# 384 bytes between the weight slots and the arena of a two-block transformer kernel

## What is computed

```python
# block 1
mod = silu(c) @ w_mod + b_mod                       # 1024 x 6144, for x and for the context
hx  = modulate(rmsnorm(x), ...);  hc = modulate(rmsnorm(ctx), ...)
q, k, v, hy = split(hx @ w_in); k_c, v_c = hc @ w_k, hc @ w_v
attn = (softmax(q1 k1) - lam * softmax(q2 k2)) @ v   # 4 heads, 768 keys
z    = hyena: two gated long convolutions by DFT matrices
x    = x + g_a * (concat(attn, z) @ w_out)
x    = x + g_f * ((gelu(conv3(h @ w_up_a)) * (h @ w_up_b)) @ w_down)      # 2816 wide
# block 2
x    = x + concat(hgrn2 both directions, mlstm both directions) @ w_out_2  # from x @ w_in_2
x    = x + cross_attention(x, mem)                                         # 4 heads, 256 keys
x    = x + relu(h @ w_up_2)**2 @ w_down_2                                  # 4096 wide
out  = rmsnorm(x)
```

## Time and profile before

| | |
|---|---|
| median of 3 runs | 1662.15 us (1659.91 to 1662.8) |
| profiled execution, first to last instruction | 1660.1 us |
| PE matmul busy | 1614.1 us, 97% |
| PE weight load busy | 1268.9 us, 76% |
| VectorE, ScalarE, GpSimd busy | 977.3, 682.4, 153.4 us |
| DMA | 173.89 MB, mean 105 GB/s |
| granted clock of TensorE, mean | 0.993 |

### The profile page before, as it was taken

The page is one execution under the profiler, slowest core; times in us unless marked ns, Lnnn a source line. Parts: engine busy times, 40 slices in busy tenths (PEclk is TensorE's granted clock), DMA queues, the critical chain, the costliest instruction groups (busy, mean ns, idle before and its releaser), DMA issues.

```text
span 1660.1 us, 18984 instructions
## 1 busy us (share of the span) xinstructions
PE 1614.1 (97%) x7258; PEld 1268.9 (76%) x7258; DVE 977.3 (59%) x1411; ACT 682.4 (41%) x1060; POOL 153.4 (9%) x155
## 2 busy tenths in 40 slices
PE   5999999999999999999999999999999999999997
PEld 1488765687788888888888787688877888888885
DVE  6986687784544424436789498675434554435262
ACT  4531465323533213325654667964433322222131
POOL 0221000252000000004000000342001000000001
PEclk9999999999999999999999999999999999999999
DMA  9543114422332232223141121444210322222231
GB/s 311 198 152 127 64 54 162 153 65 89 103 101 89 76 116 84 92 95 133 52 176 56 47 77 36 162 152 153 101 52 28 125 74 83 98 101 101 101 101 51
DMA packets 112600, 173.89 MB, mean 105 GB/s; under 512 B 3851, under 2 KB 56651, under 8 KB 112012
## 3 DMA queue, kind: packets, MB, share of 16 engines
q1 hardware_dynamic: 108220, 158.05, 28.2%
q0 software_dynamic: 4304, 14.81, 2.7%
HBM read 168.53 MB, written 4.33 MB: 104 GB/s over the span
## 4 chain that ended last, share of the span: by engine, by line
PE 84%; DVE 8%; DMA 3%; ACT 2%; issue 2%; SPq 1%; DVEq 0%; ACTq 0%
PE bank L902 17%; PE bank L904 17%; PE bank L903 17%; PE bank L939 6%; PE bank L940 6%; PE bank L944 5%; DMA weight_slots<-in_w_mod 2%; PE bank L1212 2%; PE bank L1132 1%; PE bank L1144 1%; PE bank L1342 1%; DVE weight_slots_lo L2435 1%; PE bank L1432 1%; PE bank L1407 1%; PE bank L1450 1%
## 5 line engine op out<-in xcount | busy, mean ns | idle before, releaser
L3328 POOL TENSOR_TENSOR arena<-arena 128x512 f32<-128x512 f32 (+1 forms) x56 | 76.3, 1371 | 960.3 <-ACT arena L1695 956.8
L904 PE MATMUL bank<-hx_hi,weight_slots_lo 128*128 128x512 f32 x320 | 124.8, 390 | 0.0
L3283 DVE TENSOR_TENSOR weight_slots_lo<-weight_slots,weights_hi 128x2048 fp32r<-128x2048 f32 x30 | 67.4, 2289 | 93.5 <-ACT weights_hi L2394 93.5
L2394 ACT ACTIVATE weights_hi<-weight_slots 128x2048 fp32r<-128x2048 f32 x30 | 55.8, 1908 | 160.6 <-DMA weight_slots<-in_w_up 115.9
L1664 ACT ACTIVATE weights_hi<-weight_slots 128x2048 fp32r<-128x2048 f32 (+2 forms) x46 | 77.3, 1724 | 91.7 <-DMA weight_slots<-in_ffn_w_down 57.9
L903 PE MATMUL bank<-xn_lo,weights_hi 128*128 128x512 f32 x288 | 112.0, 389 | 0.0
L902 PE MATMUL bank<-sq_hi,weights_hi 128*128 128x512 f32 x256 | 99.6, 389 | 0.0
L903 PE MATMUL bank<-sq_lo,weights_hi 128*128 128x512 f32 x256 | 99.6, 389 | 0.0
L904 PE MATMUL bank<-sq_hi,weight_slots_lo 128*128 128x512 f32 x256 | 99.6, 389 | 0.0
L1650 ACT ACTIVATE arena<-bank 128x512 f32<-128x512 f32 (+2 forms) x99 | 49.1, 532 | 96.1 <-PE bank L904 45.0
L2435 DVE TENSOR_TENSOR weight_slots_lo<-weight_slots,weights_hi 128x2048 fp32r<-128x2048 f32 (+2 forms) x34 | 65.8, 1973 | 28.1 <-ACT weights_hi L1664 28.1
(11 more groups left out here) (473 smaller groups left out, 4069.6 us busy)
## 6 DMA issues: line engine op xcount, KB each, us to landing
weight_slots<-in_w_in SPq DMA_DIRECT2D x24, 1024.0 KB, 7.3
weight_slots<-in_ffn_w_up SPq DMA_DIRECT2D x22, 1024.0 KB, 6.8
weight_slots<-in_w_up SPq DMA_DIRECT2D x16, 1024.0 KB, 6.6
weight_slots<-in_w_down SPq DMA_DIRECT2D x16, 1024.0 KB, 6.4
weight_slots<-in_w_mod SPq DMA_DIRECT2D x14, 1024.0 KB, 10.2
arena<-in_w_mod POOLq DMA_DIRECT2D x32, 256.0 KB, 3.3
weight_slots<-in_w_out SPq DMA_DIRECT2D x8, 1024.0 KB, 7.8
weight_slots<-in_w_xkv SPq DMA_DIRECT2D x8, 1024.0 KB, 7.6
```

The costliest lines, as they stand in the source:

```text
L904: return mm(ps, ll, rh, start=False, stop=stop)
L2394: A(W_hi[:, s % 2, a:b], W[:, s % 2, a:b], ACT.Copy).then_inc(w_hi, 1)
L3283: V.tensor_tensor(W_lo[:, s % 2, a:b], W[:, s % 2, a:b], W_hi[:, s % 2, a:b].bitcast(F32), ALU.subtract).then_inc(w_lo, 1)
L3328: G.tensor_tensor(acc, acc, sq[i % 2][:, 0:width], ALU.add).then_inc(sq_added, 1)
```

## The change

A tensor that nothing reads or writes is allocated between the slots and the arena. Its size is what is missing to the next multiple of 512 bytes: 128 - 128/4 = 96 words, 384 bytes.

```diff
 XH = 4
 XD = D // XH
 LEVELS = [2, 4, 8, 16, 32, 64, 128]
+PAGE = 128
...
         W_lo = nc.alloc_sbuf_tensor_at("weight_slots_lo", [P, 2, 4096], R32, offset=nc.sbuf_base - 4 * 2 * 4096)
+        sb("page_pad", [P, PAGE - nc.sbuf_base % (4 * PAGE) // 4])
         TILES = 84
         GAP, GAP_AT = 16, 78
         arena = sb("arena", [P, TILES * 512 + GAP])
```

## The result

| | before | after |
|---|---|---|
| median | 1662.47 us (1659.91 to 1663.62, 4 runs) | 1680.01 us (1679.58 to 1680.93, 4 runs) |
| profiled execution | only its span is shown | 1679.77 us |
| its span | 1660.1 us | 1678.0 us |
| TensorE's mean granted clock | 0.993 | 0.994 |

A forecast was written before the change was run, and what follows sets the result against it. PE, busy for 97% of the span, was taken to bound the kernel, with the loads of the first 50 us. All terms were 0: 1660.1 us profiled, plus 2.05 us to the median, forecast as 1662.0 us, range 1650 to 1695.

The forecast's parts named there:

- Split matmuls: PE's split matmuls, 2080 of 5736 given a new operand distance of 128 or -128: 0, between -28 and +33 us.
- The other argument: For split matmuls: earlier displaced operands were off by 64, the shift is 3 x 128, so any 128 bytes stay unchanged; 0.
- The slower rival: Low weights from the slot against an arena operand, every split product: 1640 triples x 0.020 = 33 us, 1694 us; chance 0.26.
- The smaller form of it: Same split products: displacing every third operand costs two thirds as much as displacing two in three, 1684 us.
- The faster rival: Arena operands at a multiple of 512 are read faster, saving some of 13.3 ns per matmul: 1648 us; chance 0.16.
- Other engines: VectorE instructions on shifted operands, such as the low split of 2048 words: 0, any few per cent hidden by PE.
- Clock: Granted clock of 0.97 from 1220 to 1280 us: one such dip more or less, +-1.8 us, taken as 0.
- Loads: DMA loads into the arena at the start, about 4 MB: taken as 0, bounds -2.0 and +2.0 us.
- The rule of the Trainium skill that I set against the 0: Arena loads: transfer pieces start at 256-byte boundaries, so loads get about 4 beats in 70 cheaper, estimated -0.5 us.
- My argument that 13 ns of a packet could fall away: Arena loads: 13 ns per packet don't depend on size; aligning might save 1.2 us (2 KB packets) and 0.8 us (1 KB).
- The other rule: PE's SBUF reads: PE never waits for anyone, separate ports for moving operand and weight load; 0 at any address.

## Why the prediction was wrong

**The term that failed** is "Split matmuls", taken at 0 between bounds of -28 and +33 us. It measured +21.5 us in the matmuls; 17.9 are left in the span, and 17.5 between the medians. The bounds held it; the choice between them did not. The step was this: "What repeats every 128 bytes is the simplest pattern that agrees with both." The two observations were that 64 bytes cost, and that multiples of 512 do not. A period of 128 and one of 256 (or 512) agree with both equally well, and the next sentences of the text say so. Simplicity was the only thing between them, and the runs show a period of 256: distances of 0 and 256 at 0.680 us per triple; 32, 64, 128 and 384 at 0.69 and above. The other argument, that what stands in any 128 bytes stays as it was, presumed the same period.

**The slower rival**, the distance between slot and arena, had the place, the engine, the absence of idle time and the count of the last stretch (1160 matmuls expected, 1170 measured) nearly right. Its price was too high: 0.020 us per triple, against 13.3 ns. The smaller form of it (two thirds, 1684) is the one that came nearest, at 4 us off. The two thirds fit a rule which the prediction lacked: an interval pays if its own or the next stationary operand is displaced. In the keys of before, two of three operands are, so all three intervals pay, 0.020; in the change one of three is, so two pay, 0.0133. 1640 triples at 0.0133 are 21.8 us, and the intervals compared one by one gave 21.5. The rule is read from distances of 128 and 384. The gate product doesn't follow it: there one operand alone, 64 bytes off, costs the 20 ns that the prediction read, on its own interval and the three behind it (236, 229, 232 and 231 ns), and the interval ahead of it pays nothing. How the price is shared out at 64 bytes stays open.

**What the matmuls hand on.** The rival's price let 32 of 33 us pass to the end, 97%. Of 21.5 us some 2 went mostly where PE waits for others, so about 90% passed; the rest of the difference is the 0.9 us of the start and the 0.7 us of the clock.

**The faster rival**, the arena at a multiple of 512: wrong. The 226.7 ns are the same at arena remainders of 0, 128, 256 and 384, as long as the distance is a multiple of 256.

**Other engines**: right. VectorE's split of 2048 words takes 2289 ns in the mean, as in the earlier trace rows, and the small gains of busy time are hidden. **Clock**: taken at 0 within +-1.8 us. The dip of 1220 to 1280 us is the same, a shorter one near 420 us gave 0.7 us back.

**Loads**: taken at 0 within +-2.0 us; measured -0.9 at 73 us, little more than the scatter of the start. The rule of the Trainium skill that I set against the 0 (DMA: Bandwidth & Descriptors, "How a descriptor splits into AXI transactions") was nearer. It counts beats fetched in vain when a descriptor doesn't start at a 256-byte boundary. Worked out exactly from the page, as an estimate, a 2 KB packet at a remainder of 128 has 68 beats and an aligned one 64, so 4 in 68, which would be 6.2% more packets; my 4 in 70 was rounded. The runs show 5.7% more packets in a full stretch where slots and arena are aligned, 2% where the arena alone is, and that 256 suffices. My argument that 13 ns of a packet could fall away gave the wrong quantity: 4.8 ns did (88.8 to 84.0 ns the packet of 2 KB, in the same stretch).

**The other rule** of the Trainium skill, that PE never waits for anyone at SBUF and has two read ports of its own (SBUF — State Buffer, "Who interferes with whom"), speaks of other engines. On that the runs agree: DMA at 1 or at 92 GB/s leaves the pace alone. (In the keys of before DMA was a little busier than in the loops, 96 against at most 89 GB/s, and not "not busier" as the prediction reads the earlier trace rows; with the keys' distance gone the same matmuls are fast.) But it gave 0 for this change, and the runs contradict that use of it: with the addresses of weights and moving operand apart by 128 bytes an interval grows from 226.7 to 232.5 or 234.2 ns, so PE's own two reads don't look independent. Where they would meet, no run shows. It was cited beside a trace that already disagreed, and I should have let the trace weigh more.

## What to carry to other kernels

Before a pad or a new tensor goes between two buffers that feed one matmul, compare their start addresses modulo 256: what counted in this kernel's stream of 512-column float32r matmuls was the distance between moving and stationary operand, not the alignment of either. Put both at multiples of 256, and the DMA loads gain as well (84.0 in place of 88.8 ns for a packet of 2 KB here). When a trace shows that one displacement costs, and the change makes another one on thousands of instructions, the likeliest reading is that it costs too; a period that has not been seen is no ground for a zero.

## What the runs showed that I had not expected

- The pace of a 512-column float32r matmul in this stream depends on the address of the weights that are loaded *beside* it. In steady triples: 226.7 ns with none displaced, 232.5 with the next stationary operand displaced by 128, 234.2 with its own. This is a relation of two addresses modulo 256; the arena was seen fast at remainders of 0, 128, 256 and 384 over 512, the slots at 0, 128 and 256.
- The price doesn't grow with the distance: constant 32 and 128 bytes give 1159 matmuls each in 270 us of the last loop, and 32.2 and 28.1 us over the kernel; 64 bytes between slot and arena cost 11.8 ns a triple, 128 and 384 cost 13.3. A distance of 512 between slots and arena wasn't tried in a kernel of its own; within the slabs it occurs and is free.
- Packets of 2 KB into SBUF took 88.8 ns in a full queue at a remainder of 128, and 84.0 ns at 0 or 256, 387 against 409 GB/s.
- What the 13 ns above 512 columns are at a distance of 0 stays open; no address tried here changed them. So does the mechanism behind the 256 bytes: the runs give the period and the price, and nothing of what collides.
